# A four-block transformer kernel: input tiles released one by one, statistics, convolution and pooling sums moved between evacuations

## The reference, cut to what matters

```python
for l in range(2):                                  # blocks 1 and 2
    x = x + mixer_l(rmsnorm(x, norm_mix[l]))        # l0: gated recurrence and 31-tap conv
    x = x + cross_attention(rmsnorm(x, norm_xattn[l]), rmsnorm(mem, mem_norm), ...)
    x = x + swiglu(rmsnorm(x, norm_ffn[l]), ...)
# block 4: h = rmsnorm(x, norm_g_3); p = h @ w_in_3
qk = silu(causal_four_tap_conv(p[aq, ak]))          # queries and keys of the mLSTM, 16 tiles
i, f = p[ai] + b_i, logsigmoid(p[af] + b_f)         # its gates: running sums and maxima
u = p[cu]                                           # pooling branch, four groups of 256 columns
d_g = mean of the last w tokens of u_g, minus u_g   # w = 2, 4, 8, 16
y_C = silu(p[cz]) * (pool_scale * (d_g @ pool_w_g))
```

## Time and profile before

| | |
|---|---|
| median of three runs | 4275.85 us (4275.1 to 4279.85) |
| the profiled execution: its time | 4266.35 us |
| its span | 4264.4 us |
| TensorE busy | 3814.2 us, 89% |
| VectorE, ScalarE, GpSimd busy | 1306.8, 1214.7, 1289.1 us |
| mean granted TensorE clock | 0.902 of 2.4 GHz |

### The profile page before, as it was taken

One profiled execution on the slowest core, in us unless ns is written; L12 is line 12 of the kernel. 1 busy time (PEld: TensorE's weight loads), 2 busy tenths in 40 slices (PEclk: granted clock), 3 DMA queues, 4 the chain that ended last, 5 costly groups with the idle time before them and its releaser, 6 DMA issues. The chain is left out here.

```text
span 4264.4 us, 40008 instructions
## 1 busy us (share of the span) xinstructions
PE 3814.2 (89%) x16772; PEld 3014.6 (71%) x16772; DVE 1306.8 (31%) x2033; ACT 1214.7 (28%) x1780; POOL 1289.1 (30%) x531
## 2 busy tenths in 40 slices
PE   7869999999998999989968888999886989999967
PEld 6657688875776888756757767788775668657856
DVE  5953411123234211222543224101332231132142
ACT  3333322233233223322331112322423322222222
POOL 3423244431242444211420003344233214304422
PEclk9989999997899999868977669999998989889988
DMA  3212123221121333211310012222221102202221
GB/s 132 94 50 79 55 94 99 95 86 40 53 96 50 99 95 98 76 45 42 104 65 1 1 47 89 79 95 99 79 79 64 55 30 95 74 6 89 95 78 64
DMA packets 82812, 305.36 MB, mean 72 GB/s; under 512 B 8997, under 2 KB 10825, under 8 KB 81354
## 3 DMA queue, kind: packets, MB, share of 16 engines
q1 hardware_dynamic: 78368, 280.61, 20.2%
q10 hardware_dynamic: 4266, 22.21, 1.3%
HBM read 291.77 MB, written 11.02 MB: 71 GB/s over the span
## 5 line engine op out<-in xcount | busy, mean ns | idle before, releaser
L2337 POOL TENSOR_TENSOR WL<-RW,WH 128x1024 fp32r<-128x1024 f32 x527 | 1288.9, 2448 | 2942.9 <-ACT WH L261 2942.9
L266 PE MATMUL PS<-XH,WH 128*128 128x512 f32 x2968 | 1178.5, 397 | 124.6 <-POOL WL L2337 43.0
L267 PE MATMUL PS<-XL,WH 128*128 128x512 f32 x2968 | 1169.0, 394 | 0.0
L268 PE MATMUL PS<-XH,WL 128*128 128x512 f32 x2968 | 1167.8, 393 | 0.0
L261 ACT ACTIVATE WH<-RW 128x1024 fp32r<-128x1024 f32 x527 | 552.3, 1052 | 870.4 <-PE PS L268 709.3
L266 PEld LDWEIGHTS PS<-XH,WH 128*128 128x128 f32 x2968 | 566.7, 191 | 259.7 <-POOL WL L2337 64.7
L267 PEld LDWEIGHTS PS<-XL,WH 128*128 128x128 f32 x2968 | 567.2, 191 | 118.4 <-issue 1.4
L268 PEld LDWEIGHTS PS<-XH,WL 128*128 128x128 f32 x2968 | 565.6, 191 | 119.2
L266 PE MATMUL PS<-YH,WH 128*128 128x512 f32 (+1 forms) x928 | 353.1, 381 | 57.8 <-DVE YL L753 39.0
L267 PE MATMUL PS<-YL,WH 128*128 128x512 f32 (+1 forms) x928 | 351.5, 379 | 0.0
L268 PE MATMUL PS<-YH,WL 128*128 128x512 f32 (+1 forms) x928 | 351.4, 379 | 0.0
(11 more groups left out here) (425 smaller groups left out, 3636.4 us busy)
## 6 DMA issues: line engine op xcount, KB each, us to landing
RW<-in_units SPq DMA_DIRECT2D x527, 512.0 KB, 3.3
spill<-X ACTq DMA_DIRECT2D x2, 2048.0 KB, 6.9
X<-spill ACTq DMA_DIRECT2D x2, 2048.0 KB, 8.2
X<-in_xT SPq DMA_DIRECT2D x8, 256.0 KB, 6.2
A<-spill ACTq DMA_DIRECT2D x1, 2048.0 KB, 10.4
out_T<-X ACTq DMA_DIRECT2D x1, 2048.0 KB, 7.4
spill<-X ACTq DMA_DIRECT2D x1, 1536.0 KB, 5.1
spill_gates<-X ACTq DMA_DIRECT2D x1, 1536.0 KB, 6.1
```

The source lines that it names most:

```text
L266: mm(out, hi, xh, start=first, stop=False)
L267: mm(out, hi, xl, start=False, stop=False)
L268: return mm(out, lo, xh, start=False, stop=last)
L2337: nc.gpsimd.tensor_tensor(WL[:, u % SPLIT, :], RW[:, u % RAW, :], WH[:, u % SPLIT, :].bitcast(F32), ALU.subtract).then_inc(split_done, 1)
```

## The change

1. `pe_release` is new: in the last tile of a residual layer with a norm behind it (`then`), TensorE signals after each of the first seven input tiles k that XH and XL tile k are free. The norm's ScalarE step waits for these instead of for the end of the layer. Before VectorE's evacuation of the last tile it writes the norm's XL tiles 0 to 3. For that last tile ScalarE no longer waits, and the high part of the third unit ahead moves behind the norm's steps. It applies to `l0.out`, `x0.o`, `l1.out`, `x1.o`.
2. The memory's root mean square moves from ahead of `l0.q` to behind it.
3. `l1.qk` has the partition sum after its second tile instead of its first (`rstd_at=2`).
4. `t.gif` keeps its one unit only; `t.qk` opens the norm after its second tile, and VectorE takes the gates' rows out before its own first evacuation. The four-tap convolution of a pair of tiles runs after each odd evacuation of `t.qk`, its Silu on ScalarE at the odd tile two later; the gates' work comes after `t.qk`, and the Silu of the last pair after `t.v`.
5. The window sums and the low parts of their split stand between the evacuations of `t.cz` (windows 2, 4, 8 after tiles 0, 1, 2; low parts 0 to 3 after tile 3; window 16 after tile 4; low parts 4 to 7 after tile 6), the high parts on ScalarE after tiles 2 and 5. `t.pool` writes its first unit into banks 4 to 7, without waiting for the evacuations of `t.cz`, and its first four tiles are evacuated when its first unit is done.

```diff
+        def pe_release(pe, st, u, e, name, xh, xl):
+            st.wait_ge(split_done, u + 1)
+            bank_free(st, e)
+            for k in range(KT):
+                c = slice(k * P, (k + 1) * P)
+                last = unit_passes(bank(e % 4), WH[:, u % SPLIT, c], WL[:, u % SPLIT, c], xh[:, k, :], xl[:, k, :], k == 0, k == KT - 1)
+                if k < KT - 1:
+                    st.do(last, f"{name}.free{k}")
+            last.then_inc(unit_done, 1)
...
@@ Linear.scalar
-                    elif self.squares is not None and j <= self.summing:
+                    elif self.squares is not None and j < self.summing:
                         st.wait_ge(*reached(f"ev{e}"))
-                        if j < self.summing:
-                            st.do(nc.scalar.activation(T(self.squares + j), X[:, j, :], ACT.Square), f"{self.name}.sq{j}")
-                    w_hi(act, st, u + SPLIT)
+                        st.do(nc.scalar.activation(T(self.squares + j), X[:, j, :], ACT.Square), f"{self.name}.sq{j}")
+                    if j < self.n - 1 or self.then is None:
+                        w_hi(act, st, u + SPLIT)
+                    if self.between_act is not None:
+                        self.between_act(st, j)
...
@@ Linear.vector
+                    if j == KT - 1 and self.then is not None:
+                        for k in range(4):
+                            self.then.lo_dve(dve, st, k)
                     st.wait_ge(unit_done, self.u0 + j + 1)
...
@@ Late.scalar
-                if self.after is not None:
-                    st.wait_ge(unit_done, self.after)
                 for k in range(KT):
+                    if self.after is not None and k < KT - 1:
+                        st.wait_ge(*reached(f"{self.after}.free{k}"))
...
-        Stage(tensor=lambda pe, st, e: mem.rstd_pe(pe, st), scalar=lambda act, st, e: mem.rstd_act(act, st),
-              vector=lambda dve, st, e: mem.rstd_dve(dve, st))
...
         Linear("l0.q", dst=at(8), func=ACT.Silu, late=n0, between=lambda st, j: conv(st, 1))
+        Stage(tensor=lambda pe, st, e: mem.rstd_pe(pe, st), scalar=lambda act, st, e: mem.rstd_act(act, st),
+              vector=lambda dve, st, e: mem.rstd_dve(dve, st))
...
-        Linear("l1.qk", dst=at(12), ready="n1", first=1, late=n1)
+        Linear("l1.qk", dst=at(12), ready="n1", late=n1, rstd_at=2)
...
+        def conv3(st, j):
+            if j % 2:
+                k = j - 1
+                st.settle()
+                depthwise(st, lambda q: T(k + q), lambda q: T(16 + k + q), 4, "conv_w3", None, 2, k)
+                names[f"conv3.{k}"] = (vector_steps, st.n)
+
+        def qk_silu(st, k):
+            st.wait_ge(*reached(f"conv3.{k}"))
+            st.do(a_.activation(W2(16 + k, 2), W2(16 + k, 2), ACT.Silu), "ml.qk")
+
+        def qk_act(st, j):
+            if j % 2 and j >= 3:
+                qk_silu(st, j - 3)
+        Linear("t.qk", dst=at(0), late=tn, opening=True, rstd_at=2, opened=gif_take, between=conv3, between_act=qk_act)
...
+        TokenMajor("t.v", 2, lambda h, t: T(2 * t + h), late=tn, pre=["conv3.14"])
...
+        def pool_between(st, j):
+            if j in (0, 1, 2, 4):
+                pool_window(st, (0, 1, 2, None, 3)[j])
+            elif j == 3:
+                pool_lo(st, range(4))
+            elif j == 6:
+                pool_lo(st, range(4, KT))
+
+        def pool_hi(st, j):
+            if j in (2, 5):
+                st.wait_ge(*reached(f"pool.d{1 if j == 2 else 3}"))
+                for k in range(0 if j == 2 else 4, 4 if j == 2 else KT):
+                    st.do(a_.activation(YH[:, k, :], T(16 + k), ACT.Copy), f"pd.hi{k}")
+        Linear("t.cz", dst=lambda j: X[:, j, :], func=ACT.Silu, late=tn, between=pool_between, between_act=pool_hi)
...
@@ pool_act
-            st.wait_ge(unit_done, U0["t.pool"] + 2)
             for k in range(KT):
-                st.do(a_.activation(T(8 + k), bank(k), ACT.Copy, scale=vec("pool_scale", k)), f"ev{e + k}")
+                st.wait_ge(unit_done, U0["t.pool"] + 1 + k // 4)
+                st.do(a_.activation(T(8 + k), bank((k + 4) % 8), ACT.Copy, scale=vec("pool_scale", k)), f"ev{e + k}")
```

More of the change, by code:

```diff
@@ L315, in opens @@
             def opens(self):
-                return self.late is not None and self.ready == self.late.id
+                return self.late is not None and (self.ready == self.late.id or self.opening)
             def tensor(self, pe, st):
[L319 to L323, removed]
+                for j in range(self.n):
+                    if j == 0 and self.ready is not None:
+                        pe_start(pe, st, self.ready, self.u0, self.e0, [(self.xh, self.xl)], self.cols)
+                    elif j == self.n - 1 and self.then is not None:
+                        pe_release(pe, st, self.u0 + j, self.e0 + j, self.name, self.xh, self.xl)
+                    else:
+                        pe_tile(pe, st, self.u0 + j, self.e0 + j, self.xh, self.xl, self.cols)
+                    if self.opens() and j + 1 == self.rstd_at:
                         self.late.rstd_pe(pe, st)
-                for j in range(first, self.n):
-                    pe_tile(pe, st, self.u0 + j, self.e0 + j, self.xh, self.xl, self.cols)
             def scalar(self, act, st):
+                if self.ready is not None or self.opens():
+                    w_hi(act, st, self.u0 + SPLIT - 1 + (self.rstd_at - 1 if self.opens() else 0))
+                if self.opens():
+                    self.late.rstd_act(act, st)
                 if self.add is None:
@@ L364, in vector @@
                         self.late.rstd_dve(dve, st)
+                    if self.opened is not None:
+                        self.opened(st)
                     st.wait(*self.pre)
@@ L1040, in xattn @@
         def xattn(l):
-            x = late(f"xn{l}", f"norm_xattn{l}", ready=lambda k: f"ev{mix[l].e0 + k}", after=mix[l].u0 + KT, left=[KT - 1], sq=lambda i: T(20 + i))
+            x = late(f"xn{l}", f"norm_xattn{l}", ready=lambda k: f"ev{mix[l].e0 + k}", after=mix[l].name, left=[KT - 1], sq=lambda i: T(20 + i))
+            mix[l].then = x
             Linear(f"x{l}.q", dst=at(20), ready=f"xn{l}", late=x)
@@ L2248, in pool_windows @@
-            st.do(v.memset(SM[:, 0:1], 0.0), "pool.d")
-        Linear("t.cz", dst=lambda j: X[:, j, :], func=ACT.Silu, late=tn)
-        Stage(vector=lambda dve, st, e: (drained(st, e - KT), pool_windows(st)))
-        split("pd", [T(16 + k) for k in range(KT)], YH, YL, ready=lambda k: "pool.d")
+                    st.do(v.tensor_tensor(dst[q][:, sh:], src[q][:, sh:], src[q][:, :S - sh], ALU.add))
+                    st.do(v.tensor_copy(dst[q][:, :sh], src[q][:, :sh]))
+                src = dst
@@ new lines, in pool_window @@
+            w = 2 << g
+            st.settle()
+            for q in range(2):
+                k = 2 * g + q
+                o = T(16 + k)
+                st.do(v.scalar_tensor_tensor(out=o[:, 16:], in0=src[q][:, 16:], scalar=1.0 / w, in1=T(k)[:, 16:],
+                                             op0=ALU.mult, op1=ALU.subtract))
+                st.do(v.tensor_tensor(o[:, :16], src[q][:, :16], cst("icnt", k=16 * k, n=16), ALU.mult))
+            st.settle()
+            for q in range(2):
+                k = 2 * g + q
+                st.do(v.tensor_tensor(T(16 + k)[:, :16], T(16 + k)[:, :16], T(k)[:, :16], ALU.subtract), f"pool.d{g}")
```

93 lines of the change are left out of this document (35 added, 58 removed).

## The result

The changed kernel takes **4169.9 us** (median, 4168.9 to 4174.3), the kernel before in the same set 4277.9 (4275.1 to 4281.2): ratio 0.9749, 95% interval 0.9732 to 0.9766, 107.9 us less. In later sets the two took 4170.1 and 4276.8 to 4279.4. The forecast was 4182 in a range of 4157 to 4207. From profiled execution to profiled execution the time fell from 4266.35 to 4174.3, by 92.1 us, where the sum of the terms said 93.6. So two things have to be explained: whether the parts are what the terms say, and where the other 16 us between the medians are.

The account below looks back on a forecast made before the run. TensorE, busy 89% of the span, was taken as the bound, so edits were worth the TensorE waits removed. Terms summed to 93.6 us: 4172.8 from the profiled 4266.35, 4182 against the median 4275.85; range 4157 to 4207.

Parts of the forecast that it names:

- four releases: At `x0.q`, `x1.q` and both up-projections the partition sum starts earlier, 4.1 us each, 16.4 in all.
- memory's root: Ahead of `l0.q`: saves VectorE's idle time ahead of the reciprocal, 3 us, bounds 0 and 9.
- `l1.qk`: Second tile fills TensorE's wait for the last sum; third tile starts earlier: 7 us, bounds 5 and 9.3.
- gates, `t.qk`, `t.v`: Units run on at the gates, 14.2 us; convolution beside `t.qk` shrinks the stops up to `t.v`, 30.8 us.
- pooling: Windows within `t.cz` cut TensorE's stop from 30.3 to 9.8 us; `t.br2` starts 22.2 us earlier, bounds 12 and 28.
- the last sum of a released norm: Caught behind GpSimd's operation on the third unit, so the partition sum starts at 372.3, not 376.4.
- the lag of the convolution: In `t.qk` VectorE keeps pace but late, pair m ending at 3105.5+10.9m; TensorE stops 7.2 us at `t.v`.
- A: Port costs more: `t.qk`'s lag grows 1.4 us a pair, pooling gives 12 instead of 22; 4203 us, chance 0.21.
- B: Less is caught behind GpSimd, lag at `t.v` 1.7 us, clock holds, pooling 6 better; 4158 us, chance 0.17.
- C: Releases start the next unit earlier, but the norm's end stays; 16.4 and 7 lost; 4205 us, chance 0.08.
- D: In `t.qk` and `t.cz` late splits pause TensorE every unit, clock stays at 1.2 GHz; 4313 us, chance 0.04.
- the exempt case: VectorE's single-input operations escape the port shared with GpSimd; the forecast sum would be about 1 us lower.

Follow-up runs that it names:

- root first: Changed kernel with ScalarE taking the root ahead of the third unit's weight high half at the four released norms: 4161.6 us.
- the three moves together: Changed kernel with root ahead of that split, last two convolution pairs behind `t.qk` with Silus behind `t.v`, and windows between `t.cu`'s evacuations: 4148.6 us.

## Why the prediction was right, and where it was not

| term | forecast us | step in the traces | medians |
|---|---|---|---|
| four releases | 16.4 | 15.5 | 19.1 |
| memory's root | 3 | 4.1 at 94 us, 2.9 at 283 us | 2.9 and 10.5 |
| `l1.qk` | 7 | 7.5 | 8.8 |
| gates, `t.qk`, `t.v` | 45.0 | 44 to 46 | 48.8 |
| pooling | 22.2 | 23.3 | 26.2 |
| sum | 93.6 | 93 to 96 | 106 (with 2.9) |

**The parts.** Each term is within 1.5 us of its step; for the memory's root that holds at the two places only, and its worth at the end is open. The two steps of the working that carried most are seen in the rows. One is that VectorE's SBUF work stands still for each GpSimd operation: the last sum of a released norm was forecast to be caught, with "some 2 us" ahead of the partition sum, and is, by 1.7; root first, which only takes GpSimd away from there, brings them back. The other is the lag of the convolution: pair by pair VectorE takes 10.7 us (from the evacuations at 3132.92 to those at 3143.62) where I had 10.9, and TensorE's stop at `t.v` is 7.43 for 7.2. The stop at `t.pool` is 8.80 for 9.8, `t.br2` 23 us earlier for 22.2. Rivals A, B, C and D fall with that: the port cost what I took, the sums were caught, each release gave 3 to 4.5 us, and the clock was 0.98 in `t.qk` and 1.00 in `t.cz`.

**Misreadings inside it.** I said that the convolution's L1122 would show a mean of 1 us beside `t.qk`; L1142, as it is now, shows 1.4 (6 in 8.54 us). My own pair sum had that (5.1 and 4.8 to 5.3 us for eight operations is 1.2 to 1.3); the sentence on what to look for forgot it. The releases' gap was not wholly due to the wait for the end of the unit: 0.66 of its 4.93 us were ScalarE's wait for the last evacuation, ahead of its split. And at `n1` I had the third GpSimd operation right (the six sums take 10.61 us where they took 8.46; I had 11), but forecast one wait of 3.1 us for the last sum, where there are two, 1.29 for a weight and 1.23 for the sum.

**The step that failed** is the last one: "it was 9.5 us below the median of the runs, so against the median 4275.85: 4182". Carried out on profiles, the sum gives 4172.8, and the profiled execution took 4174.3. I carried the 9.5 us over unchanged, as if they were a constant of measuring (4275.85 less 93.6 is the same 4182). They are not. The second profile of before is 14.7 us longer than the first, and the surplus lies inside the program, at places where nothing differs in the code. The typical execution of before loses these microseconds; the changed kernel's two profiles are 2 apart and 2 to 4 above its median, so it has no such surplus, and the medians stand 107.9 apart where the two first profiles stand 92.1. In the same way an undone part costs up to 5 us more by its medians than by its step in one trace. The pages show what the differences are made of (us; idle is the span less TensorE's busy time; matmul ends are modelled, in the same way in every profile):

| profile | span | TensorE busy | idle | mean clock |
|---|---|---|---|---|
| before | 4264.4 | 3814.2 | 450.2 | 0.902 |
| before, again | 4278.9 | 3824.1 | 454.8 | 0.899 |
| changed | 4172.2 | 3803.4 | 368.8 | 0.911 |
| changed, again | 4170.2 | 3800.3 | 369.9 | 0.911 |
| memory part undone | 4185.8 | 3816.8 | 369.0 | 0.908 |
| memory part undone, again | 4170.7 | 3801.3 | 369.4 | 0.911 |

The two profiles with the memory part undone are 15.1 us apart with the same idle time: all of it is the same 16772 matmuls taking longer at a lower mean clock. So from before to changed, 81 to 85 us are waits that went, and the rest, 11 us between the first profiles and 24 between the second ones, is TensorE's own work taking less time. The sum of the terms, 93.6, fits the 92.2 us between the first two. The second two are 108.7 apart, near the medians' 107.9, by 3.5 us more of waits and 13.0 more of TensorE's busy time: the sum prices the clock only behind a stop, and took the rest as the same in every execution. Why the clock's falls cost the kernel before more in its typical execution stays open: no run here sets the clock apart from the stops.

**What the scatter is**, as far as seen: places where the clock falls in one execution and not in the next. In the attention section ("MoBA" in the expectations) heads follow each other with the same instructions. Two heads of the changed kernel:

```profile
1032.77:1042.67 9.90, 8.18 (x34) 4.41 (x35) 5.46 (x18) 3.95 (x13) 0.00 (x0) 0.96 0.01 2
1042.67:1055.51 12.84, 11.12 (x35) 5.68 (x35) 5.48 (x18) 4.01 (x13) 0.00 (x0) 0.76 0.00 0
```

and two of the kernel before, in its first profile:

```profile
1036.07:1048.87 12.80, 11.09 (x34) 5.68 (x35) 5.47 (x18) 4.00 (x13) 0.00 (x0) 0.77 0.00 0
1060.40:1070.30 9.90, 8.19 (x34) 4.41 (x35) 5.28 (x18) 3.95 (x13) 0.00 (x0) 1.00 0.00 0
```

A head costs 9.9 us at the upper level (granted clock 0.96 to 1.00) and 12.8 where the clock is 0.76 or 0.77, so an execution takes this section in portions of 3 us. Which heads pay differs from one execution to the next; what decides it was not tried. Root first is 3.2 us earlier at 1067 than at 878 us with no edit near; the three moves together are 1.5 later at 1067, and by 1169 1.3 earlier than at 878.

## What to carry to other kernels

Work that is moved off the path beside another engine has to be costed with the port: here VectorE's SBUF work was lengthened by one GpSimd operation for each that ran, and with that one price the stop after 16 tiles came out within 0.3 us. Where a moved piece leaves a stop, ask which of its parts the waiting engine really needs: in all three stops left here the answer (a root ahead of a split, two convolution pairs behind the last evacuation, windows one layer earlier) gave 8 to 10 us each. And profile the kernel before twice before reading a difference of 3 us at one place: matched instruction by instruction, two traces of one kernel were up to 5 us apart there, and 14.7 at the end.

## What the runs showed of the hardware that was not expected

- VectorE's single-input operations are caught as well. Two of 0.44 us (L1136; 0.88 for two at 3144.93, with GpSimd idle) took 5.02 us from 3068.00 beside GpSimd's 3067.80 to 3072.73, rows above. That was left open in the prediction, and the "about 1 us lower" of the exempt case falls. The Trainium skill, SBUF — State Buffer, "SBUF: two separate sides", says it of single-input operations in a two-port mode; the trace agrees on these two.
- When ScalarE hands GpSimd one split after the other, GpSimd's operations follow with gaps of 0.48 us in the changed kernel (0.05 to 0.50 in the others), and VectorE gets about one operation into each: four of 0.7 us took 9.0 to 11.1 us in `x0.k` in all fourteen profiles. TensorE's longest wait for VectorE there is 7.3 where they took 9.0 or 9.1, and 8.2 to 8.3 where they took 10.4 or 11.1, the first profile of before (10.2, and 4.94 with the pause shown above) aside. No run took that stop away.
- One set of a kernel can centre several us off: with the memory part undone it was 4180.4 (spread over 13 us) and 4173.0 (over 2 us), and the profiles of the two sets differ in TensorE's busy time, not in its waits.
